# Diagonals of the row maxima built by ScalarE in place of VectorE, in a four-layer transformer kernel

## The reference

```
s = where(mask, q @ k.T * scale + bias, -inf)
p = exp(s - rowmax(s)) / sum(exp(s - rowmax(s)))     # SWA: the sink takes part in the max and the sum
o = p @ v
```

## Time and profile before

| | |
|---|---|
| median of three runs | 2652.36 us |
| the profiled execution | 2649.54 us |
| its span, first to last instruction | 2647.8 us |
| instructions | 28561 |
| PE busy | 2423.0 us, 92% |
| DVE busy | 1710.8 us, 65% |
| ACT busy | 298.5 us, 11% |
| POOL busy | 1502.4 us, 57% |
| mean granted TensorE clock | 0.95 of full speed |

### The profile page before, as it was taken

The page is one execution under the profiler, slowest core; times in us unless marked ns, Lnnn a source line. Parts: engine busy times, 40 slices in busy tenths (PEclk is TensorE's granted clock), DMA queues, the critical chain, the costliest instruction groups (busy, mean ns, idle before and its releaser), DMA issues.

```text
span 2647.8 us, 28561 instructions
## 1 busy us (share of the span) xinstructions
PE 2423.0 (92%) x10786; PEld 1941.3 (73%) x10786; DVE 1710.8 (65%) x1654; ACT 298.5 (11%) x516; POOL 1502.4 (57%) x656
## 2 busy tenths in 40 slices
PE   5978899999997899999999778999999888899999
PEld 3666678888775677888877546888878675688887
DVE  7786677763378657776348677807867454792570
ACT  2223110000012211000000410000001132000000
POOL 3465556666546465666654564666655555465664
PEclk8988899999998899999999888999999999899999
DMA  3110122222212012222332112222232200222222
GB/s 136 63 62 1 64 79 95 95 77 97 104 48 84 1 51 88 100 95 75 99 112 80 64 48 80 95 95 96 95 111 96 80 17 16 76 99 96 95 95 80
DMA packets 37837, 207.86 MB, mean 79 GB/s; under 512 B 3532, under 2 KB 10316, under 8 KB 16888
## 3 DMA queue, kind: packets, MB, share of 16 engines
q1 hardware_dynamic: 37752, 206.70, 22.4%
HBM read 204.55 MB, written 2.13 MB: 78 GB/s over the span
## 4 chain that ended last, share of the span: by engine, by line
PE 50%; DVE 13%; ACT 2%; issue 1%; POOL 1%; DVEq 0%; ACTq 0%; POOLq 0%
PE ps L799 14%; PE ps L804 14%; PE ps L803 14%; DVE h L1597 2%; DVE ssq L1593 2%; DVE h L1601 1%; PE ps L1146 1%; DVE t L1601 1%; DVE act L1597 1%; PE ps L856 1%; PE ps L1120 1%; DVE nt L1593 1%; DVE act L1593 1%; DVE x L1593 1%; ACT sq L1282 1%
## 5 line engine op out<-in xcount | busy, mean ns | idle before, releaser
L625 POOL TENSOR_TENSOR wl<-raw,wh 128x2048 fp32r<-128x2048 f32 (+1 forms) x194 | 889.1, 4583 | 16.2
L623 POOL TENSOR_SCALAR wh<-raw 128x2048 fp32r<-128x2048 f32 (+1 forms) x194 | 363.1, 1872 | 873.1 <-PE ps L799 708.0
L799 PE MATMUL ps<-h,wh 128*128 128x512 f32 x1576 | 629.2, 399 | 53.9 <-DVE h L1601 39.5
L803 PE MATMUL ps<-h,wh 128*128 128x512 f32 x1576 | 621.2, 394 | 0.0
L804 PE MATMUL ps<-h,wl 128*128 128x512 f32 x1576 | 620.9, 394 | 0.0
L799 PE MATMUL ps<-act,wh 128*128 128x512 f32 x1120 | 442.3, 395 | 24.8 <-DVE x L1593 22.9
L804 PE MATMUL ps<-act,wl 128*128 128x512 f32 x1120 | 439.8, 393 | 0.0
L803 PE MATMUL ps<-act,wh 128*128 128x512 f32 x1120 | 439.8, 393 | 0.0
L799 PEld LDWEIGHTS ps<-h,wh 128*128 128x128 f32 x1576 | 300.9, 191 | 133.5 <-DVE h L1601 48.3
L803 PEld LDWEIGHTS ps<-h,wh 128*128 128x128 f32 x1576 | 301.3, 191 | 63.3 <-issue 2.1
L804 PEld LDWEIGHTS ps<-h,wl 128*128 128x128 f32 x1576 | 300.6, 191 | 63.3
(11 more groups left out here) (339 smaller groups left out, 2863.3 us busy)
## 6 DMA issues: line engine op xcount, KB each, us to landing
raw<-w_gu SPq DMA_DIRECT2D x44, 1024.0 KB, 4.8
raw<-w_up SPq DMA_DIRECT2D x32, 1024.0 KB, 4.8
raw<-w_down_b SPq DMA_DIRECT2D x32, 1024.0 KB, 4.9
raw<-w_down_a SPq DMA_DIRECT2D x32, 704.0 KB, 4.0
raw<-w_in_a SPq DMA_DIRECT2D x14, 1024.0 KB, 4.9
raw<-w_in_f SPq DMA_DIRECT2D x13, 1024.0 KB, 4.9
raw<-w_in_r SPq DMA_DIRECT2D x11, 1024.0 KB, 4.9
raw<-w_out_a SPq DMA_DIRECT2D x8, 1024.0 KB, 7.7
```

The costliest lines, as they stand in the source:

```text
L623: pool.tensor_scalar(hi_s, raw[s][:, 0:n], 1.0, 1.0, ALU.mult, ALU.mult).then_inc(hi_done, 1)
L625: pool.tensor_tensor(lo_s, raw[s][:, 0:n], hi_s.bitcast(F32), ALU.subtract).then_inc(w_ready, 1)
L799: first = pe.matmul(out, w_hi, v_hi, start=start, stop=False)
L803: pe.matmul(out, w_hi, v_lo, start=False, stop=False)
```

## The change

ScalarE gets a new function `diagonals(hd, half)`. It waits for the two maxima of that half and writes two blocks of `dg` as copies of the identity with the maximum as the scale. It is called for both halves of head 0 ahead of the loop; in the loop the first half of head hd+1 stands between `reciprocal(hd-2)` and `exponentials(hd)`, the second half behind `exponentials(hd)`. VectorE's line 2004 goes, and its waits for `free` in front of it outside of SWA. In SWA VectorE signals the max with the sink by a new semaphore, `max_ready`, and doesn't wait for it itself. Since VectorE may now be a head ahead of ScalarE, the maxima are kept apart for even and odd heads (`sm` grows from 32 to 40 columns). The factor -1 moves from the diagonal into the ones: `ones_r` becomes `neg_ones_r`, written at the start with scale -1.

```diff
-        mx, rtok, rtokm, csp = sm[:, 0:4], sm[:, 4:8], sm[:, 8:10], sm[:, 12:16]
+        mx = [sm[:, 0:4], sm[:, 32:36]]
...
-                        last = pe.matmul(out, ones_r[:, :], maxima, start=False, stop=m.kind == "full")
+                        last = pe.matmul(out, neg_ones_r[:, :], maxima, start=False, stop=m.kind == "full")
...
-                fn(dst[:, :], cst[:, c0:c0 + P], ACT.Copy)
+                fn(dst[:, :], cst[:, c0:c0 + P], ACT.Copy, scale=-1.0 if dst is neg_ones_r else 1.0)
...
+                def diagonals(hd, half):
+                    if m.name == "swa":
+                        sc.wait_ge(max_ready, mxr.up())
+                    elif m.kind == "causal":
+                        sc.wait_ge(free[0], bk.emptied(0, 2 * hd + half))
+                        sc.wait_ge(free[1], bk.emptied(1, 2 * hd + half))
+                    else:
+                        sc.wait_ge(free[half], bk.emptied(half, hd))
+                    for i in (0, 1) if half == 0 else (2, 3):
+                        ins = fn(dgs[m.name][hd % 2][:, i, :], ident[:, :], ACT.Copy, scale=mx[hd % 2][:, i:i + 1])
+                    if half:
+                        ins.then_inc(dg_ready, 1)
+                diagonals(0, 0)
+                diagonals(0, 1)
                 for hd in range(m.heads + 2):
                     if hd >= 2:
                         reciprocal(hd - 2)
+                    if hd + 1 < m.heads:
+                        diagonals(hd + 1, 0)
                     if hd < m.heads:
                         exponentials(hd)
+                    if hd + 1 < m.heads:
+                        diagonals(hd + 1, 1)
...
-                        dve.wait_ge(free[0], bk.emptied(0, 2 * hd + half))
-                        dve.wait_ge(free[1], bk.emptied(1, 2 * hd + half))
...
-                    if m.name == "swa":
-                        two_mx = mx[:, 2 * half:2 * half + 2]
-                        tsc(two_mx, two_mx, col(f"sink{l}", 3 * (hd % 2) + hd // 2), None, ALU.max)
-                    for i in two:
-                        ins = dve.tensor_scalar(dg[:, i, :], ident[:, :], mx[:, i:i + 1], -1.0, ALU.mult, ALU.mult)
-                        if i == TB - 1:
-                            ins.then_inc(dg_ready, 1)
-                            dgr.up()
+                        two_mx = mxs[:, 2 * half:2 * half + 2]
+                        dve.tensor_scalar(two_mx, two_mx, col(f"sink{l}", 3 * (hd % 2) + hd // 2), None,
+                                          ALU.max, ALU.bypass).then_inc(max_ready, 1)
```

More of the change, by code:

```diff
@@ L306, in build @@
         anti_r = keep("anti_r", [P], F32R)
-        ones_r = keep("ones_r", [P], F32R)
+        neg_ones_r = keep("neg_ones_r", [P], F32R)
         maskt_r = keep("maskt_r", [P], F32R)
@@ L315, in build @@
         vec = keep("vec", [N_COLS])
-        sm = keep("sm", [32])
+        sm = keep("sm", [40])
         nck = keep("nck", [4, 16])
-        mx, rtok, rtokm, csp = sm[:, 0:4], sm[:, 4:8], sm[:, 8:10], sm[:, 12:16]
+        mx = [sm[:, 0:4], sm[:, 32:36]]
+        rtok, rtokm, csp = sm[:, 4:8], sm[:, 8:10], sm[:, 12:16]
         csn = sm[:, 24:28]
@@ L440, in build @@
         norm_qk, hi_ready, qk_ready = sem("norm_qk"), sem("hi_ready"), sem("qk_ready")
-        dg_ready, mix_out = sem("dg_ready"), sem("mix_out")
+        max_ready, dg_ready, mix_out = sem("max_ready"), sem("dg_ready"), sem("mix_out")
         up_ready = sem("up_ready")
@@ L1134, in score_columns @@
                         pe.wait_ge(free[5], bk.emptied(5, hd - 1))
-                        pe.matmul(ps[5][:, :], ones_r[:, :], dg[:, :, :].rearrange("p b n -> p (b n)"),
+                        pe.matmul(ps[5][:, :], neg_ones_r[:, :], dg[:, :, :].rearrange("p b n -> p (b n)"),
                                   start=True, stop=True).then_inc(ready[5], 1)
@@ L1279, in _ @@
             op1 = Count(one_plus, kept)
+            mxr = Count(max_ready, kept)
             def fn(out, in_, f, **kw):
@@ L1311, in _ @@
             sc.wait_ge(ld_vec, 16)
-            for dst, c0 in ((ident, C_IDENT), (ones, C_ONES), (ident_r, C_IDENT), (anti_r, C_ANTI), (ones_r, C_ONES),
+            for dst, c0 in ((ident, C_IDENT), (ones, C_ONES), (ident_r, C_IDENT), (anti_r, C_ANTI), (neg_ones_r, C_ONES),
                             (maskt_r, C_MASKT), (maskq_r, C_MASKQ)):
-                fn(dst[:, :], cst[:, c0:c0 + P], ACT.Copy)
+                fn(dst[:, :], cst[:, c0:c0 + P], ACT.Copy, scale=-1.0 if dst is neg_ones_r else 1.0)
             fn(gather[:, :, :].rearrange("p a n -> p (a n)"), cst[:, C_GATHER:C_GATHER + 256], ACT.Copy)
@@ L1579, in _ @@
             nqk = Count(norm_qk, kept)
-            dgr = Count(dg_ready, kept)
             den = Count(den_ready, kept)
@@ L1978, in maxima @@
                 def maxima(hd, half):
-                    dg = dgs[m.name][hd % 2]
-                    two = (0, 1) if half == 0 else (2, 3)
+                    mxs = mx[hd % 2]
                     if m.kind == "causal":
-                        for i in two:
+                        for i in (0, 1) if half == 0 else (2, 3):
                             b, u = i % 2, 2 * hd + i // 2
                             dve.wait_ge(ready[b], bk.filled(b, u))
-                            dve.tensor_reduce(mx[:, i:i + 1], ps[b][:, 0:(i + 1) * P], AX_X, ALU.max).then_inc(free[b], 1)
-                        dve.wait_ge(free[0], bk.emptied(0, 2 * hd + half))
-                        dve.wait_ge(free[1], bk.emptied(1, 2 * hd + half))
-                    else:
[L1990 to L1998, removed]
-                        dve.wait_ge(free[b], bk.emptied(b, hd))
@@ L2000, in maxima @@
-                    if m.name == "swa":
-                        two_mx = mx[:, 2 * half:2 * half + 2]
-                        tsc(two_mx, two_mx, col(f"sink{l}", 3 * (hd % 2) + hd // 2), None, ALU.max)
-                    for i in two:
-                        ins = dve.tensor_scalar(dg[:, i, :], ident[:, :], mx[:, i:i + 1], -1.0, ALU.mult, ALU.mult)
-                        if i == TB - 1:
-                            ins.then_inc(dg_ready, 1)
-                            dgr.up()
+                            dve.tensor_reduce(mxs[:, i:i + 1], ps[b][:, 0:(i + 1) * P], AX_X, ALU.max).then_inc(free[b], 1)
@@ new lines, in maxima @@
+                        return
+                    b = half
+                    dve.wait_ge(ready[b], bk.filled(b, hd))
+                    if m.kind == "band" and b == 0:
+                        dve.tensor_reduce(mxs[:, 0:1], ps[0][:, P:256], AX_X, ALU.max).then_inc(dve_step, 1)
+                        dve.wait_ge(dve_step, chain.up())
+                        dve.tensor_reduce(mxs[:, 1:2], ps[0][:, 256:T], AX_X, ALU.max).then_inc(free[0], 1)
+                    else:
+                        dve.tensor_reduce(mxs[:, 2 * b:2 * b + 2], ps[b][:, :].rearrange("p (a c) -> p a c", a=2),
+                                          AX_X, ALU.max).then_inc(free[b], 1)
@@ L2009, in out @@
+                    if m.name == "swa":
+                        dve.wait_ge(free[b], bk.emptied(b, hd))
+                        two_mx = mxs[:, 2 * half:2 * half + 2]
+                        dve.tensor_scalar(two_mx, two_mx, col(f"sink{l}", 3 * (hd % 2) + hd // 2), None,
+                                          ALU.max, ALU.bypass).then_inc(max_ready, 1)
                 def out(hd):
```

## The result

Four runs of the changed kernel have a median of 2629.51 us (2626.67 to 2631.18), four of the kernel before 2651.06 us: the ratio is 0.9913, with a 95% interval of 0.99 to 0.9925, so 20 to 26.5 us less. The forecast was 2633.2 in a range of 2625 to 2645. The profiled execution took 2628.49 us, its span 2626.7.

What follows compares the result with a forecast made beforehand. TensorE was taken to set the time where it runs without a gap, VectorE, held up by GpSimd, elsewhere. 14.9 us from two SWA passes plus 4.3 from XA of layer R gave 19.2: 2652.4 to 2633.2 us, range 2625 to 2645.

Steps and rivals of the forecast that it cites:

- XA of R: XA of layer R: four pairs leave VectorE's unbroken chain up to the weighted sum of head 1; gain 4.3 us (2 to 6).
- SWA up to the first output product: Start of each SWA pass: gain 1.0 us at heads 0 and 1, plus 0.65 from two bare pairs leaving VectorE's queue.
- The 0.9 that I gave back to ScalarE's order: SWA head 1: ScalarE takes 2.84 us from max to columns, around head 0's exponentials, against VectorE's 1.95; 0.9 lost.
- From there to the weighted sum of head 2: SWA from the first output product: head 4's max slips into the weight split's first half; 12.2 to 8.2 us, gain 4.0.
- To the weighted sum of head 3: SWA, from head 2's weighted sum: 8.14 us loses 0.5 for a pair and 1.4 for half clock; gain 2.0.
- The rest of the pass: SWA head 5: a bare pair on the path gives 0.2 us back.
- the second rival: Nothing to be measured: other collisions, with recurrences meeting GpSimd's output splits, fill VectorE's freed time; about 4 us left, 2648; 9%.
- MLA, FOX, XA of F at 0: The four other passes: small gains at starts and losses before exponentials sum to 0 us (-1.5 to +1).
- The wait that I charged at head 4 of MLA as 0.2: MLA head 4: ScalarE's pair before the exponentials meets a gap of only 0.29 us, so 0.2 is lost.
- The signs: Trace checks: shorter diagonal waits and gaps, max about 1.2 us, SWA 52 to 53, copies 0.38; wrong if MLA/FOX waits exceed 3.
- The collision all the same: SWA: head 4's max still meets the weight split and waits as now; total gain 9.1 us, 2643.3; 20%.
- The slower one: ScalarE's order makes TensorE wait for banks 2 and 3; 22 us if nothing is covered, 13 slower net, 2665; 5%.

Runs made afterwards that it cites:

- pairs behind the exponentials: Changed kernel with both ScalarE pairs of the next head placed after this head's exponentials, instead of one pair in front of them; 2633.15 us, ratio 0.9923 to before.
- the move of the split on the kernel before: Kernel before the change, with GpSimd's weight split moved from head 3 of SWA to head 4 of MLA; 2644.08 us, ratio 0.9972.
- the idle pairs: Changed kernel, with VectorE also computing a pair of unread 128x128 products from SBUF behind each max; 2648.84 us, ratio 0.9988 to the kernel before.
- doubled pairs: Changed kernel with each of ScalarE's 80 pairs done twice, with a wait for the first in between; 2634.44 us, ratio 0.9933 to the kernel before.

## Why the prediction was right

- *The base.* The waits on diagonals alone would have given 14.6 us. It was the held-up instruction (0.89 against 0.48 us a pair) and the max of 3.91 us that led to the right places: the three passes named (SWA twice, XA of R) have the gain, the four others none.
- *SWA up to the first output product:* predicted 1.0 + 0.65. The product ended 29.76 us behind the first maximum (146.88 to 176.64) and now 28.15 (149.44 to 177.59): 1.61. The sum is right and its parts are not; that is luck. The max of head 1 comes 3.98 us earlier in the pass (11.29 in place of 15.27 behind the first maximum), not 1.9 and outside my 1.0 to 2.5. The 0.9 that I gave back to ScalarE's order doesn't show, as pairs behind the exponentials win nothing. What takes the difference is GpSimd's preparation, the 3.75 us that I didn't foresee as what comes next: without it 2.0 and 2.8 us more are won, and then ScalarE's order shows, with 3.07 us for my 2.84. In the second SWA that wait is 4.62 us, and this part wins 0.84.
- *From there to the weighted sum of head 2:* predicted 4.0 from 12.18 to 8.2, measured 7.01, so 5.17. The bound by VectorE, 7.25, was the right one; I leant to TensorE's at half clock, and the clock there was 1.00.
- *To the weighted sum of head 3:* predicted 2.0, measured 8.14 less 6.86 = 1.28. The 1.4 for the weighted sum at full clock is there (3.00 us, now 1.59), the 0.5 for the pair is not (5.14, now 5.27): TensorE still waits 0.39 us for it, on ScalarE. The two terms together are 6.45 for 6.0, and the move of the split on the kernel before measures the same collision at 5.9 and 6.4 per pass.
- *The rest of the pass:* predicted -0.2, measured 10.70 against 10.90. The second SWA, 7.11 in all, repeats the last three terms within 0.02 us.
- *XA of R:* predicted 4.3, measured 4.12. TensorE reaches the weighted sum of head 1 4.70 us earlier in the pass (its wait of the earlier trace rows is 1.75), and 0.6 is lost behind it: the last weighted sum and the matmuls with the ones behind it take 5.57 us at a mean clock of 0.56, before 4.84 at 0.64. The second recurrence still meets GpSimd's preparation, one instruction later (0.77, 1.66 and 1.64 us from 1506.10 on, before 1.67, 1.10 and 1.22). The third meets GpSimd's output splits anew, as the second rival had it: 1.13 and 1.64 us at 1513.13 and 1514.29, before 0.68 and 0.69.
- *XA of R with the idle pairs:* 1.5 us of the gain stay. The trace has 0.95 of them in the first 9 us of the pass, with the same matmuls at a mean clock of 0.80 in place of 0.65, and 0.46 in VectorE's run up to the product of head 1 (18.27 us for 18.73), where an idle pair is a little cheaper than a real one.
- *MLA, FOX, XA of F at 0:* right. The wait that I charged at head 4 of MLA as 0.2 is there with 0.28; in FOX two heads of the four have it, with 0.16 and 0.15 for my 0.1:
```profile
252.62 0.38 PE L1121 MATMUL ps<-qh,kh 128*128 128x256 f32 x1 [0.28 <-ACT pt L1284]
```
- *The sum:* 19.2 predicted, 19.2 by passes, 20 to 26.5 by the timed runs. That the first two agree to the tenth is luck, as terms off by +1.2, -0.7 and -0.8 us cancel. The difference of 2 to the timed runs is within what the clock does to single executions, and a median of four doesn't settle it.
- *The signs.* Gone or small as said: the max (1.09), the gaps at the weighted sum of head 2 in SWA (0.30) and at head 1 of XA (1.75), copies of 0.39. TensorE's waits on ScalarE in MLA and FOX are 1.5 us in all, under the 3 that would have been wrong, and no table load lies in an attention pass. Missed: the wait of 3.58 us on the diagonals of head 0 is 2.02 and that of head 5 is 1.09, not under 1, and the second SWA is 53.66, over the 52 to 53.
- *The rivals.* The collision all the same (20%) was decided by the changeover, as the prediction said, and by little: the max began 1.07 us before the first half ended. The slower one (22 us if nothing is covered) read the gaps in front of the exponentials rightly: doubled pairs are paid for in full where the gap is under 0.5 us, at the heads of MLA and FOX that it names. They are few, and there the first pair costs 0.9 us in all. Its "1.4 and more elsewhere" is wrong for SWA, where the exponentials of heads 2 to 4 follow the reciprocal without a gap (187.34 + 0.63, then 187.99 in the trace before); doubled pairs cost at most 0.8 us there, since other waits cover them.

## What to carry to other kernels

Price an instruction by its bare duration and by its held-up mean; the difference says whether moving it to another engine pays, even one that is slower by the bare figure. Then follow the queue behind it: the largest part of the gain here is one collision of 6 us in each of two passes, and it was lost when instructions that nobody needs took the place of those that had gone. Of the 160 that were moved, 96 won nothing. A transfer of work into a pass where TensorE runs through is free only until the engine's later outputs are late, as the moved split showed.

## What the runs showed of the hardware

- A VectorE instruction from SBUF that stands waiting got its turn between two instructions of GpSimd, not after both: the max at 180.76 ended at 181.85, GpSimd's next began at 181.91. One that starts in the second waits it out: the max at 181.62 in the kernel before ended at 185.53, the second half at 185.51, and the idle pair ended at 186.81, the second half at 186.73. The Trainium skill ("SBUF — State Buffer", SBUF: two separate sides) says that the pair belongs to one instruction for its whole length; the rows agree.
- Same instructions, same waits, another clock: the end of MLA took 2.42 or 4.12 us, and FOX with XA of layer F 107.6 to 107.9 us in most traces and 112.2 to 114.1 in three of the twelve experiments' ones, with a stretch at 0.50 where the others have 0.82 (the 111.4 of the doubled pairs is ScalarE's, see there). A single trace of this kernel is uncertain by 2 to 6 us for that alone, and differences below that were read by pass, not by the span.
